# Hybrid trunk kernel: the next norm made in the tail of the stage before, and decay rows of the state-space part brought by transfers

## The chip, the cores and the metric

The kernel runs on one core of a Trainium2 chip. The metric is the device time of one launch, in microseconds. The engines are named as in the profile: PE is TensorE, DVE is VectorE, ACT is ScalarE, POOL is GpSimd and SP issues transfers. P is 128 partitions and T is 512 tokens. Activations lie with the features on partitions, so that one "tile" of the residual is 128 features by 512 tokens, and the model width of 1024 is DK = 8 tiles.

## The reference

Two layers of a trunk on 512 tokens of 1024 features, all in fp32. Layer 0 mixes by a state-space part (SSD, 16 heads) beside windowed attention, layer 1 by an mLSTM. Each mixer is followed by an expert layer (`peer`) and a gated embedding:

```python
for i in range(DEPTH):                       # 2
    h = rmsnorm(x, norm_mix[i])
    x = x + (even_mixer if i % 2 == 0 else mlstm_mixer)(h, ...)
    x = x + peer(rmsnorm(x, norm_ffn[i]), pk_w_q[i], ..., pk_u[i], pk_v[i])
    gate = sigmoid(rmsnorm(x, norm_ple[i]) @ ple_gate[i])
    x = x + gate * (p[i] @ ple_w[i])
return rmsnorm(x, norm_final)
```

A norm is `x * rsqrt(mean(x*x) + eps) * g`. In the SSD part the kernel uses the quadratic form over all 512 tokens: for each head n the weights are `exp(cum[t] - cum[s])` for s <= t, times the product of the state inputs, and `y` is these weights times `x * dt`. `cum` is the running sum of the head's decay, one row of 512 numbers per head.

## The kernel before

**Units.** Every fp32 product is made of three products of halves: a value is split into `hi` (rounded) and `lo` (the rest). One unit is a weight block of 128x1024: SP loads it (`w_raw`), ACT makes `w_hi` (`split_hi`, L157), DVE or POOL makes `w_lo` (L163, L170), and PE multiplies it with the activation's halves in 24 matmuls of 512 columns (`product`, L184). Two split buffers let the halves of the next unit be made while PE works on this one.

**Blocks.** The program is a chain of blocks (`together`), each with a barrier of all engines at its end: the start; EvenFront with EvenSSD; the expert layer of layer 0 (TopK, Decode, Gates, Values, Ple); OddMixer; the expert layer of layer 1, which ends in the final norm. Within a block each engine runs its part of the stages in written order; waits are on counted semaphores.

**Norms.** `Norm` works tile by tile: `act_tile` makes the `hi` of x times the gain (L295) and the square (L300), `dve_tile` the `lo` (L312). The sum of squares over features is a matmul with ones: per tile (`pe_sum`, L324), or POOL adds the tiles (`pool_sums`, L333) and PE does one (`pe_total`, L339). Then `act_root` scales the sum (L305) and takes the square root (L307), and DVE takes the reciprocal (L318). The scale is applied to a unit's result, so that PE's units don't wait for it. TopK, OddMixer and the first block begin with `pe_unit`: unit 0, where each of the 8 tiles waits for its `lo` and is followed by the sum of the tile before. All of this stands at the head of the block, after the barrier.

**EvenSSD.** Sixteen heads are worked in pairs, one pair c per step `it` of a loop from -1 to 8. For each head n of pair it+1: PE spreads row n of `decay_rows` (16x512) over 128 partitions by a matmul with a column of the identity (L808, into PSUM bank n % 2, after the exps of head n-2); DVE takes its minimum with a column (L946, into `q`); ACT makes ten exps of 128x128 with a bias, six from the PSUM row (L867) and four from the minimum (L871), into one of R = 3 buffers `ssd_weights`. PE then transposes x of pair it+1 (L814) for `x_dt` (DVE, L961). For `it` in 0 to 4 and 8 PE does one output unit of the attention part (`UNIT_AT`; ACT and DVE make the halves of the unit after it). DVE multiplies the exps of the pair `it` with the mask product (L955, 128x1280), PE does the pair's product (L827, 2 heads x 4 matmuls), DVE adds and gates it (L971, L973), ACT squares it and makes its hi (L879, L880), and PE adds the square by a matmul with ones (L834). Then come root and reciprocal, and the last eight output units, each followed by DVE's scaling (L990) and addition to the residual (L992).

## Time and profile before

| | us |
|---|---|
| median of 3 runs | 4336.39 (4335.25 to 4337.31) |
| the profiled execution | 4336.64 |
| its span in the trace | 4335.1 |
| PE busy in it | 4245.1 (98%) |
| DVE busy in it | 2735.5 (63%) |
| ACT busy in it | 2065.7 (48%) |
| POOL busy in it | 1270.8 (29%) |
| one `w_hi` on ACT (L157, mean of 694) | 1.059 |
| one `w_lo` on DVE (L163, mean of 585) | 1.230 |

The granted clock of PE over the span is 0.99 of full speed. PE has work almost all the time, so the span is made of PE's matmuls and of the few places in which PE waits or runs at the lower clock. Those places are the SSD loop (about 299 to 411 us) and the heads of the blocks (TopK of layer 0 at 457, OddMixer at 2104, TopK of layer 1 at 2670, the final norm at 4312).

### The profile page before, as it was taken

The page shows a single profiled execution, that of the slowest core. Times are in us where ns is not written, and L with a number is a line of the kernel's source. Part 1 is how long each engine was busy: PE and PEld are TensorE (multiplying, and loading weights), DVE is VectorE, ACT ScalarE, POOL GpSimd, SP SyncE. Part 2 cuts the span into 40 slices and gives each one's busy share as a digit, 9 for nine tenths or more (in the row PEclk, how much of TensorE's full clock was granted, in tenths as well). Part 3 has the DMA queues.
Part 4 walks back from the last instruction along what each step waited for, and adds up shares of the span by engine and source line. Part 5 has one row for each costly group of instructions (what it writes and reads, how often), then busy time and mean ns, then how long its engine had stood idle before and what let it go on. Part 6 is the DMA issues. An engine that isn't in the chain of part 4 may idle for free. (4 is left out here: it accounts for less than half of the span.)

```text
span 4335.1 us, 61169 instructions
## 1 busy us (share of the span) xinstructions
PE 4245.1 (98%) x19253; PEld 3441.9 (79%) x19253; DVE 2735.5 (63%) x5672; ACT 2065.7 (48%) x4035; POOL 1270.8 (29%) x1592
## 2 busy tenths in 40 slices
PE   8999999999999999999899999999999999999998
PEld 6665787888888888888688887888888888888886
DVE  3646799677774444444677774997777744444445
ACT  3744333677773333333455553334778743333334
POOL 0300245777770000001100000446888720000002
PEclk9989999999999999999999999999999999999999
DMA  3111233555557555552222222335555575555532
GB/s 113 59 44 40 97 111 135 206 185 181 202 207 253 195 191 196 186 201 97 71 84 85 87 82 90 112 124 175 204 181 203 184 270 193 195 190 194 193 136 83
DMA packets 180220, 654.06 MB, mean 151 GB/s; under 512 B 17424, under 2 KB 17552, under 8 KB 175200
## 3 DMA queue, kind: packets, MB, share of 16 engines
q1 hardware_dynamic: 102960, 371.41, 25.3%
q0 software_dynamic: 40240, 213.69, 13.9%
q10 hardware_dynamic: 36864, 67.13, 4.1%
q8 instruction: 68, 1.11, 0.1%
q14 instruction: 88, 0.72, 0.1%
HBM read 507.42 MB, written 144.74 MB: 150 GB/s over the span
## 5 line engine op out<-in xcount | busy, mean ns | idle before, releaser
L184 PE MATMUL ps<-h_hi,w_hi 128*128 128x512 f32 x4104 | 1621.1, 395 | 38.2 <-DVE h_lo L312 17.8
L184 PE MATMUL ps<-h_hi,w_lo 128*128 128x512 f32 x4104 | 1601.9, 390 | 0.0
L184 PE MATMUL ps<-h_lo,w_hi 128*128 128x512 f32 x4104 | 1601.6, 390 | 0.0
L163 DVE TENSOR_TENSOR w_lo<-w_raw,w_hi 128x1024 fp32r<-128x1024 f32 x585 | 719.3, 1230 | 1089.9 <-ACT w_hi L157 1085.5
L157 ACT ACTIVATE w_hi<-w_raw 128x1024 fp32r<-128x1024 f32 x694 | 734.8, 1059 | 1029.6 <-PE ps L184 878.2
L184 PEld LDWEIGHTS ps<-h_hi,w_hi 128*128 128x128 f32 x4104 | 771.9, 188 | 213.6 <-issue 40.3
L184 PEld LDWEIGHTS ps<-h_hi,w_lo 128*128 128x128 f32 x4104 | 771.8, 188 | 164.1
L184 PEld LDWEIGHTS ps<-h_lo,w_hi 128*128 128x128 f32 x4104 | 772.3, 188 | 154.9 <-issue 4.3
L1490 POOL TENSOR_SCALAR second_hot<-iota,token_keys 128x128 fp32r<-128x128 f32 x1024 | 723.7, 722 | 0.0
L184 PE MATMUL ps<-y_hi,w_hi 128*128 128x512 f32 x1344 | 534.1, 397 | 12.2 <-DVE y_lo L312 10.3
L1528 ACT ACTIVATE first_scaled<-first_hot,token_keys 128x128 fp32r<-128x128 f32 x1792 | 539.4, 388 | 3.2 <-issue 2.6
L184 PE MATMUL ps<-y_lo,w_hi 128*128 128x512 f32 x1344 | 525.8, 391 | 0.0
L184 PE MATMUL ps<-y_hi,w_lo 128*128 128x512 f32 x1344 | 525.7, 391 | 0.0
L170 POOL TENSOR_TENSOR w_lo<-w_raw,w_hi 128x1024 fp32r<-128x1024 f32 x109 | 279.8, 2567 | 699.2 <-ACT w_hi L157 699.2
L1599 POOL DMA_DIRECT2D gelu_block<-acts x30 | 26.5, 883 | 1188.4 <-DVE y_lo L1626 612.4
L184 PEld LDWEIGHTS ps<-y_hi,w_hi 128*128 128x128 f32 x1344 | 254.2, 189 | 72.5 <-issue 11.4
L1438 DVE TENSOR_REDUCE gate_group<-ps 128x512 f32<-128x1024 f32 x256 | 302.6, 1216 | 6.3 <-PE ps L1509 6.3
L1459 DVE TENSOR_SCALAR first_hot<-iota,token_keys 128x128 f32<-128x128 f32 x1024 | 242.1, 303 | 91.2 <-PE ps L1509 51.7
L184 PEld LDWEIGHTS ps<-y_lo,w_hi 128*128 128x128 f32 x1344 | 254.0, 189 | 56.0 <-issue 4.0
L184 PEld LDWEIGHTS ps<-y_hi,w_lo 128*128 128x128 f32 x1344 | 253.8, 189 | 53.3
L1021 ACT ACTIVATE gelu<-ps 128x512 f32<-128x512 f32 x256 | 151.1, 590 | 281.7 <-PE ps L184 281.3
L1609 ACT ACTIVATE h_hi<-gelu_block 128x512 fp32r<-128x512 f32 x128 | 81.0, 633 | 251.9 <-DVE gelu_block L1621 251.9
(333 smaller groups left out, 3562.6 us busy)
## 6 DMA issues: line engine op xcount, KB each, us to landing
w_raw<-in_u SPq DMA_DIRECT2D x256, 512.0 KB, 3.3
w_raw<-in_v SPq DMA_DIRECT2D x256, 512.0 KB, 3.3
gates<-gate_group POOLq DMA_DIRECT2D x36, 2048.0 KB, 8.3
acts<-gelu ACTq DMA_DIRECT2D x256, 256.0 KB, 2.1
gate_block<-gates POOLq DMA_DIRECT2D x32, 2048.0 KB, 17.8
gelu_block<-acts POOLq DMA_DIRECT2D x30, 2048.0 KB, 11.4
w_raw<-in_od_in SPq DMA_DIRECT2D x65, 512.0 KB, 3.2
w_raw<-in_ev_in SPq DMA_DIRECT2D x33, 512.0 KB, 3.3
```

Source lines behind the costliest of these rows:

```text
L157: self.nc.scalar.activation(self.wh[:, slot % SPL, :], self.raw[:, slot, :], ACT.Copy).then_inc(self.sig("w_hi_ready").sem, 1)
L163: self.nc.vector.tensor_tensor(self.wl[:, slot % SPL, :], self.raw[:, slot, :], self.wh[:, slot % SPL, :].bitcast(F32), ALU.subtract).then ...
L170: self.nc.gpsimd.tensor_tensor(self.wl[:, slot % SPL, :], self.raw[:, slot, :], self.wh[:, slot % SPL, :].bitcast(F32), ALU.subtract).then ...
L184: ins = self.nc.tensor.matmul(out, a[:, s, w], b[:, k, :], start=first and j == 0 and m == 0, stop=last and j == n - 1 and m == 2)
L1021: p.nc.scalar.activation(self.ga[:, s, :], p.ps[:, s, :], ACT.Gelu).then_inc(self.ge.sem, 1)
L1438: v.tensor_reduce(gb[:, half, :, at:at + 4].rearrange("p a t -> p t a"), self.bank(q).rearrange("p t c a -> p t a c"), AX_X, ALU.add).then ...
L1459: ins = v.tensor_scalar(o1[:, t % R1, :], p.iota[:, :], self.key(0, t), None, ALU.is_equal)
L1490: ins = p.nc.gpsimd.tensor_scalar(self.o2[:, t % self.R, :], p.iota[:, :], self.key(1, t), None, ALU.is_equal)
L1528: ins = p.nc.scalar.activation(self.os[:, t % self.R, c, :], self.o1[:, t % self.R1, :], ACT.Copy, scale=self.key(2 + c, t))
L1599: pool.dma_start(at[:, 1 - s, :, :], rows[:, bass.ds(i * B + B, B), :]).then_inc(bl[1 - s].sem, 16)
L1609: self.p.nc.scalar.activation(self.halves[s][0][:, j, :], self.at[:, s, j, :], ACT.Copy).then_inc(self.ah.sem, 1)
```

## The change

**Seams.** The tiles of the next norm are made in the tail of the block before it: as soon as the residual's tile is final, ACT makes its `hi` and square, DVE its `lo`, POOL adds the square to a total, and PE does one matmul with ones at the end of the block. This goes for EvenSSD (norm of expert layer 0), Ple of layer 0 (norm of the mLSTM) and OddMixer (norm of expert layer 1). The next block begins with a plain `product` and `act_root`. Since `hi` and `lo` are written while the block's last units still read the other pair, layer 1 swaps the pairs h and y.

**Root.** `act_root` makes a dummy square root of a column of ones ahead of its wait, in all norms.

**Decay rows.** Only heads 0 and 1 are still spread by PE. POOL writes `decay_rows` to DRAM, and loads each row n >= 2 spread over 128 partitions into a ring of four tiles of `xbc` that are free by then. Rows 2 to 5 are loaded at once, row n >= 6 after the exps of head n-4. DVE's minimum and ACT's six exps read the row from SBUF. The squares of the SSD output are summed on POOL, and PE does one matmul with ones at the end, not eight.

```diff
@@ Norm
     def act_root(self, act):
         a, ps = self.p.nc.scalar, self.p.ps
+        a.activation(self.p.spare[:, :], self.p.ones[:, 0:1], ACT.Sqrt)
         act.wait_ge(self.ss.sem, self.ss.at(DK))
@@ EvenSSD
+    def row(self, n):
+        return self.p.ps[:, n, :] if n < 2 else self.b["xbc"][:, 8 + n % self.RING, CONV - 1:]
@@ EvenSSD.gpsimd
+        pool.wait_ge(self.rc.sem, self.rc.at(1))
+        pool.dma_start(self.held, self.cum[:, :]).then_inc(self.kept.sem, 16)
+        pool.wait_ge(self.kept.sem, self.kept.at(16))
+        def load(n):
+            if n >= 2 + self.RING:
+                pool.wait_ge(self.ex.sem, self.ex.at(n - self.RING + 1))
+            pool.dma_start(self.row(n), self.held[n:n + 1, :].to_broadcast([P, T])
+                           ).then_inc(self.loaded[n % self.RING].sem, 16)
+        pool.wait_ge(self.cb.sem, self.cb.at(2))
+        for n in (2, 3):
+            load(n)
+        for it in range(DK + 1):
+            for n in (2 * it + 4, 2 * it + 5):
+                if n < HEADS:
+                    load(n)
+            c = it - 1
+            if c >= 1:
+                pool.wait_ge(self.sq.sem, self.sq.at(c + 1))
+                if c > 1:
+                    pool.wait_ge(self.sa.sem, self.sa.at(c - 1))
+                g.tensor_tensor(self.total, self.s2[:, 0, :] if c == 1 else self.total,
+                                self.s2[:, c % 2, :], ALU.add).then_inc(self.sa.sem, 1)
+        pool.wait_ge(self.osc.sem, self.osc.at(1))
+        self.after.pool_sums(pool)
@@ EvenSSD.tensor
                 for n in (2 * c, 2 * c + 1):
-                    if n >= 2:
-                        pe.wait_ge(self.ex.sem, self.ex.at(n - 1))
-                    t.matmul(p.ps[:, n % 2, :], p.ident[0:H, n:n + 1].to_broadcast([H, P]), self.cum[:, :],
-                             start=True, stop=True).then_inc(self.sp.sem, 1)
+                    if n < 2:
+                        t.matmul(self.row(n), ...).then_inc(self.sp.sem, 1)
...
-            for c in ((it - 2,) if it < DK else (it - 2, it - 1)):
-                if c >= 0:
-                    pe.wait_ge(self.sq.sem, self.sq.at(c + 1))
-                    t.matmul(p.ps[:, 3, :], p.ones[:, :], self.s2[:, c % 2, :], start=c == 0, stop=c == DK - 1
-                             ).then_inc(self.ss.sem, 1)
+        pe.wait_ge(self.sa.sem, self.sa.at(DK - 1))
+        t.matmul(p.ps[:, 3, :], p.ones[:, :], self.total, start=True, stop=True).then_inc(self.ss.sem, 1)
         pe.wait_ge(self.zl.sem, self.zl.at(DK))
         for k in range(DK, 2 * DK):
             unit(k)
+        self.after.pe_total(pe)
@@ EvenSSD.scalar
-                                         p.ps[:, n % 2, j * P:(j + 1) * P], ACT.Exp,
+                                         self.row(n)[:, j * P:(j + 1) * P], ACT.Exp,
...
+            act.wait_ge(self.osc.sem, self.osc.at(k - DK))
+            self.after.act_tile(act, k - 1 - DK)
@@ EvenSSD.vector
+                        got = self.loaded[n % self.RING]
+                        dve.wait_ge(got.sem, got.at(16 * ((n - 2) // self.RING + 1)))
                         dve.wait_ge(self.ex.sem, self.ex.at(n - 1))
...
+            if i:
+                self.after.dve_tile(dve, i - 1)
             dve.wait_ge(used.sem, u0 + k + 1)
@@ TopK.tensor
-        self.norm.pe_unit(pe, u0, p.ps[:, 4, :])
-        for n in range(1, L):
-            query(u0 + n, (u0 + n) % RAW, 4 + n, (p.yh, p.yl))
+        for n in range(L):
+            query(u0 + n, (u0 + n) % RAW, 4 + n, (self.norm.hi, self.norm.lo))
@@ TopK.scalar
-        for k in range(DK):
-            self.norm.act_tile(act, k)
-            if k == 3:
-                split(1)
+        split(1)
         self.norm.act_root(act)
@@ Ple.scalar
-            if self.final and i:
+            if i:
                 act.wait_ge(self.ad.sem, self.ad.at(i))
                 self.last.act_tile(act, i - 1)
@@ Ple.vector
+            if i >= 2 and not self.final:
+                self.last.dve_tile(dve, i - 2)
@@ OddMixer.tensor
-        self.norm.pe_unit(pe, self.u0, p.ps[:, 7, :])
+        p.product(pe, self.u0, self.u0 % RAW, p.ps[:, 7, :], p.hh, p.hl).then_inc(used.sem, 1)
...
+        self.after.pe_total(pe)
```

On PE, in a step of the SSD loop of the kernel before, between the products of one pair (L827) and the next output unit (L184):

```order
L827 MATMUL ps<-ssd_weights,x_dt 64x512
L827 MATMUL ps<-ssd_weights,x_dt 64x384
L827 MATMUL ps<-ssd_weights,x_dt 64x256
L827 MATMUL ps<-ssd_weights,x_dt 64x128
L808 MATMUL ps<-decay_rows,ident 128x512 x2
L814 MATMUL ps<-ident,xbc 128x128 x4
L184 MATMUL ps<-y_hi,w_hi 128x512
```

The same place of the changed kernel:

```order
L864 MATMUL ps<-ssd_weights,x_dt 64x512
L864 MATMUL ps<-ssd_weights,x_dt 64x384
L864 MATMUL ps<-ssd_weights,x_dt 64x256
L864 MATMUL ps<-ssd_weights,x_dt 64x128
L851 MATMUL ps<-ident,xbc 128x128 x4
L185 MATMUL ps<-y_hi,w_hi 128x512
```

The two spreads (L808) are gone, and with them PE's wait for the exps; nothing else changed places.

On POOL, before, from the SSD part's two small steps to the end of the block (the branches are the barrier):

```order
L756 COPY incl_centred<-incl 128x128 [waits ssd_turned]
L758 TENSOR_TENSOR incl_centred<-incl_centred,ones 64x128 [waits ssd_centred]
L191 UNCONDITIONAL_BRANCH
L207 UNCONDITIONAL_BRANCH [waits barrier_Pool_Activation_PE_DVE_SP_gather]
L1178 UNCONDITIONAL_BRANCH
```

And in the changed kernel, where L772 is the write of the rows to DRAM, L778 are the loads, L793 the adds of the SSD output's squares and L335 those of the next norm:

```order
L770 TENSOR_TENSOR incl_centred<-incl_centred,ones 64x128 [waits ssd_centred]
L772 DMA gates<-decay_rows 16x512 [waits ssd_rows]
L778 DMA xbc<-gates 128x512 [waits ssd_cb,ssd_rows_kept]
L778 DMA xbc<-gates 128x512 x3
L778 DMA xbc<-gates 128x512 [waits ssd_exp] x4
L793 TENSOR_TENSOR q<-squares 128x512 [waits ssd_squares]
L778 DMA xbc<-gates 128x512 [waits ssd_exp] x2
L793 TENSOR_TENSOR q<-q,squares 128x512 [waits ssd_squares_added,ssd_squares]
L778 DMA xbc<-gates 128x512 [waits ssd_exp] x2
```

An idle engine got a queue in which the loads of a pair stand behind the add of an earlier pair's square.

On PE at the seam into TopK of layer 0, before (the branches are the barrier; `pair_sums` holds the squares):

```order
L184 MATMUL ps<-h_hi,w_lo 128x512
L191 UNCONDITIONAL_BRANCH
L197 UNCONDITIONAL_BRANCH
L184 MATMUL ps<-y_hi,w_hi 128x512
L184 MATMUL ps<-y_lo,w_hi 128x512
L184 MATMUL ps<-y_hi,w_lo 128x512
L324 MATMUL ps<-pair_sums,ones 128x512
```

And in the changed kernel:

```order
L185 MATMUL ps<-h_hi,w_lo 128x512
L341 MATMUL ps<-q,ones 128x512
L192 UNCONDITIONAL_BRANCH
L198 UNCONDITIONAL_BRANCH
L185 MATMUL ps<-y_hi,w_hi 128x512
L185 MATMUL ps<-y_lo,w_hi 128x512
L185 MATMUL ps<-y_hi,w_lo 128x512
```

The eight sums of one tile each, which stood between the matmuls of the block's unit 0, became one, ahead of the barrier.

## Rows read from the trace of the kernel before

**Rows 1.** The page's groups: op, shape, count | busy, mean ns | PE's idle time before, releaser.

```profile
L184 PE MATMUL ps<-h_hi,w_hi 128*128 128x512 f32 x4104 | 1621.1, 395 | 38.2 <-DVE h_lo L312 17.8
```

**Rows 2.** Timeline of PE, 311 to 383 us: start, duration, instructions [idle before <-releaser].

```profile
311.11 0.78 PE L184 MATMUL ps<-y_hi,w_hi 128*128 128x512 f32 x1
...
319.19 3.93 PE L827 MATMUL ps<-ssd_weights,x_dt 128*64 128x512 f32 x16
...
365.11 1.98 PE L808 MATMUL ps<-decay_rows,ident 16*128 16x512 f32 x4
367.02 0.66 PE L814 MATMUL ps<-ident,xbc 128*128 128x128 f32 x4
...
382.25 6.71 PE L827 MATMUL ps<-ssd_weights,x_dt 128*64 128x512 f32 x16 [1.69 <-DVE ssd_weights L955]
```

**Rows 3.** PE by windows from one L827 to a next: us, busy (instructions), clock, DMA.

```profile
333.25:347.30 14.05, 13.70 (x49) 0.88 0.12 38
...
360.20:373.08 12.88, 12.88 (x51) 1.00 0.13 41
373.08:382.25 9.17, 7.48 (x28) 0.94 0.00 0
382.25:394.19 11.94, 10.26 (x26) 0.76 0.00 0
394.19:400.75 6.56, 6.56 (x19) 0.74 0.00 0
```

**Rows 4.** Timeline of ACT, exps of head 0, and of DVE, `x_dt` of pair 0.

```profile
302.77 1.66 ACT L867 ACTIVATE ssd_weights<-ps,decay_biases 128x128 f32<-128x128 f32 x6
304.29 1.30 ACT L871 ACTIVATE ssd_weights<-q,decay_biases 128x128 f32<-128x128 f32 x4
```

```profile
303.36 0.75 DVE L961 TENSOR_TENSOR x_dt<-ps,dt_cols 128x256 f32<-128x256 f32 x2 [0.35 <-PE ps L814]
```

**Rows 5.** The tile ssd_weights: ns min/median/max, first and last start.

```profile
L955 DVE TENSOR_TENSOR ssd_weights<-ssd_weights,q x16: 1479/1484/1493, 312.2 to 401.1; 128x1280 f32<-128x1280 f32 x16
```

**Rows 6.** Landing of OddMixer's row loads (tile od_row), and the page's gate_block loads.

```profile
DMA to landing us min/median/max: 3.2/3.3/4.4
```

```profile
gate_block<-gates POOLq DMA_DIRECT2D x32, 2048.0 KB, 17.8
```

**Rows 7.** Timeline at the seam into TopK of layer 0.

```profile
457.52 0.69 DVE L992 TENSOR_TENSOR residual<-ssd_out,residual 128x512 f32<-128x512 f32 x1
...
460.68 0.77 PE L184 MATMUL ps<-y_hi,w_hi 128*128 128x512 f32 x1 [3.92 <-DVE y_lo L312]
...
477.95 0.60 ACT L305 ACTIVATE peer_scores_left<-ps 128x512 f32<-128x512 f32 x1 [2.46 <-PE ps L324]
```

**Rows 8.** Timeline at the seam into OddMixer, then PE's waits of 2126 to 2160.

```profile
2109.27 0.77 PE L184 MATMUL ps<-h_hi,w_hi 128*128 128x512 f32 x1 [5.34 <-DVE h_lo L312]
...
2126.59 0.60 ACT L305 ACTIVATE rstd<-ps 128x512 f32<-128x512 f32 x1 [2.49 <-PE ps L324]
```

```profile
PE ps L184 <- POOL w_lo L170: 3.9, 2, 3.3
```

**Rows 9.** Timeline at the seam into TopK of layer 1.

```profile
2673.31 0.47 PE L184 MATMUL ps<-y_hi,w_hi 128*128 128x512 f32 x1 [3.26 <-DVE y_lo L312]
...
2687.87 0.60 ACT L305 ACTIVATE peer_scores_left<-ps 128x512 f32<-128x512 f32 x1 [2.48 <-PE ps L324]
```

**Rows 10.** Timeline of the final norm.

```profile
4319.00 2.05 PE L339 MATMUL ps<-squares_total,ones 128*128 128x512 f32 x2 [6.19 <-POOL squares_total L333]
...
4321.70 1.28 ACT L307 ACT_TABLE_LOAD   x1
```

**Rows 11.** Lines L1359 (DVE, two SBUF inputs) and L333 (POOL add): ns min/median/max.

```profile
L1359 DVE TENSOR_TENSOR pos_equal<-pos_float,iota x16: 2291/2293/4373, 696.3 to 2965.1; 128x2048 f32<-128x2048 f32 x16
```

```profile
L333 POOL TENSOR_TENSOR squares_total<-squares_total,squares x18: 1260/1852/1857, 2023.5 to 4317.6; 128x512 f32<-128x512 f32 x18
```

More of the change, by code:

```diff
@@ L1038, with __init__ @@
     N = 4 * PEER_HEADS + 4
-    def __init__(self, p, b, rows, wq, us, sub, gain, nxt, ctx):
+    def __init__(self, p, b, rows, wq, us, sub, before, hn, nxt, ctx):
         H = PEER_HEADS
@@ L1708, with __init__ @@
     EMB_AT = 5
-    def __init__(self, p, values, emb, gate, gain, nxt, ctx, final=None):
+    def __init__(self, p, values, emb, gate, gain, pairs, nxt, ctx, final=None, then=None):
         self.p, self.values, self.src, self.gate, self.nxt, self.final = p, values, emb, gate, nxt, final
@@ L1721, in __init__ @@
         self.ld, self.hi, self.lo, self.et, self.sc, self.si, self.mu, self.ad = (Mark(p.sig(n), k) for n, k in counts)
+        if then:
+            self.last = Norm(p, then, pairs[1], 6, scratch=(self.norm.s2, None), total=total)
         if final:
@@ L2131, in scalar @@
         hi(HEADS, 1, DK - 1)
-        for k in range(2, 2 * DK):
-            ahead(k)
+        for k in range(2, 2 * DK + 1):
+            if k < 2 * DK:
+                ahead(k)
+            half, q = OUT_UNITS[k - 1]
+            if half == 1:
+                act.wait_ge(self.added.sem, self.added.at(q + 1))
+                self.after.act_tile(act, q)
     def vector(self, dve):
@@ L2225, in weigh @@
                           ).then_inc(self.vs.sem, 1)
-        for k in range(DK):
-            self.norm.dve_tile(dve, k)
         self.norm.dve_root(dve)
@@ L2317, in ffn_firsts, with ffn @@
     return firsts(d[f"wq{layer}"])
-def ffn(p, layer, nxt, final=None):
+def ffn(p, layer, before, hn, nxt, final=None, then=None):
     d = p.dram
```

119 lines of the change are left out of this document (68 added, 51 removed).

## Prediction, made before the changed kernel ran

> **What bounds the kernel now.** First the table of the profile: PE is busy 98% of the span, so only two kinds of time can go: matmuls that are no longer there or run at a higher clock, and waits of PE. The page's costliest group [rows 1], PE's units, says what the longest wait is for: of its 38.2 us of idle time, 17.8 are spent on `h_lo`, the half that the next norm makes at the head of a block. The change works on three seams, the final norm and the SSD loop, which I read apart.
>
> In the SSD loop the timeline of PE [rows 2] and its windows [rows 3] show the period from one pair's products to the next: 14.05 us for two steps, 12.9 for two, then 9.2, 11.9, 6.6 and 4.7. The first four hold an output unit and PE is busy in 13.7 of 14.05 and in all of 12.9: PE itself is the bound. In the next two PE idles 1.7 us each and runs at a clock of 0.94 and 0.76 of full speed. At the lower of its two levels (1.2 against 2.4 GHz, granted 0.5) the pair's product takes 6.71 us in place of 3.93 [rows 2].
>
> **SSD loop, PE's part.** A spread pair takes 1.91 us warm (365.11 to 367.02 in [rows 2]), the product 3.86 (3.93 less its overlap), the transposes 0.66, and a unit 24 x 0.227 = 5.45, the rest of the 12.88 of a step with spread and square sum [rows 3]: 3.86 + 1.91 + 0.66 + 5.45 = 11.88, and 1.0 for the square's matmul. Without the spreads and the sum, PE's step is 3.86 + 0.66 + 5.45 = 10.0 us.
>
> **SSD loop, the chain behind it.** Three weight buffers mean that a head's exps wait for the product of the head three before. The way round is: half a product 1.95, handoff 0.5, ten exps, the square and hi of ACT (1.3, two operations of 0.6 and 0.7), `w_hi` 1.06, `w_lo` 1.23 (table of the profile) and the multiplication 1.48 [rows 5]. The exps: six of the PSUM row cost 1.52 us from start to start [rows 4], 0.25 each; four from SBUF come to about 1.16, 0.29 each. Six from SBUF cost 6 x 0.04 = 0.24 more, so 2.95 in all. Sum 1.95 + 0.5 + 2.95 + 1.3 + 1.06 + 1.23 + 1.48 = 10.5, of which ACT's hi and DVE's work partly overlap: I take 10.2. PE and chain are level, so the four steps with units become 10.1 each: 53.9 (twice 14.05 and twice 12.9) less 40.4 = 13.5 us gained.
>
> The steps without a unit (three of them, and the last with less): ACT needs 2 x 2.95 + 1.3 = 7.2, and DVE with two multiplications, x_dt and five operations of 128x512 (0.7 each, as in [rows 7]) about the same. I take 7.5, 7.5, 6.0 and 4.0 in place of 9.15, 11.95, 6.55 and 4.7: 7.35. The head of the loop: unit 2 starts at 311.11 behind the spreads of heads 2 and 3 [rows 2]. Afterwards only x_dt of pair 0 holds the transposes of pair 1: it ends at 304.1 [rows 4], they 0.6 later, so that the unit can start at 304.7, 6.4 earlier; 6 of it I count, since the unit is cold and DVE's multiplications stand behind the exps. One sum of squares less at the end: 1.0. Together 6 + 13.5 + 7.35 + 1.0 = 27.9.
>
> **What the loop gives back.** PE will idle 3 of 7.5 us in steps 5 to 7, where it idled 1.7 of 9.2 and 11.9 and the clock had already fallen to 0.74 to 0.94. I expect the lower level from there through the unit behind the loop: product 6.7 + transposes 1.1 = 7.8, slightly above the chain's 7.5, and about 5 us on units 7 and 8. That is 6 us. Second, POOL now adds squares (1.26 to 1.86 us each, median 1.85 [rows 11]), and DVE's minimum reads the row from SBUF. The same rows show a DVE operation with two SBUF inputs at 2.29 us and once 4.37 beside POOL. One such wait a step on part of eight steps: 1.3 us. So the loop gives 27.9 - 7.3 = 20.6; bounds 13 (cold in the steps with units as well) and 27 (no clock loss).
>
> The Trainium skill ("SBUF — State Buffer", section "Who interferes with whom") says that a DVE instruction with two SBUF inputs contends with a GpSimd instruction that reads SBUF, and that the lock is exclusive. The row of 4.37 agrees. By that rule each of 14 minima could wait out a whole POOL add, 14 x 1.2 = 17 us; since only one of 16 instances in the row shows it in full and a POOL add fills 1.3 to 1.9 of 7.5 to 10 us, I keep 1.3.
>
> **The new wait.** DVE now waits for a row's landing, and with it its multiplications, x_dt and gating, then ACT's exps and PE. The loads of OddMixer are of the same shape (one DRAM row over 128 partitions, 256 KB) and land in 3.2 to 4.4 us [rows 6]. A row n is asked for after the exps of head n-4 and used after those of n-2, a pair later: 10 us in the steps with a unit, 7.5 without. POOL's queue puts the add of a square ahead of the loads, so there remain some 7 us: enough, but by 1 to 2 us only for the last pairs. I count nothing, and up to 2 us in the range.
>
> **Seams.** The way over each seam after: last residual tile, ACT hi and square 1.3, POOL add 1.3 to 1.9, ones matmul 1.0 warm or 2.05 cold, barrier 0.6, unit 5.45 warm, 7.5 cold for its first part. Seam 1: today the residual is ready at 457.52 + 0.69 = 458.2 and unit 0 with its sums is over at 477.95 [rows 7]: 19.7 us. After: 1.3 + 1.5 + 2.05 + 0.6 + 7.5 = 13.0 (POOL idle, so that only the last add counts): gain 6.7, taken as 6.5. Seam 2: from the last matmul, 5.34 of wait and 2126.59 - 2109.27 = 17.3 [rows 8], 22.7 us. After, the final norm is the model, which already works in this way: 6.19 of wait and 2.05 for the matmul [rows 10], 0.7 more for hi, 0.6 and 7.5: 17.0, gain 5.7. Here the root is ready some 13 us earlier too, and POOL's `w_lo` no longer holds PE for 3.9 us [rows 8] (this is work behind ACT, whose root and table load come late today); I count 3.3 of it. Seam 2: 9.0. Seam 3: 3.26 + 14.56 = 17.8 today at full clock [rows 9]; after, 0.8 for the eviction + 1.3 + 1.6 + 1.5 + 0.6 + 6.7 (between warm and cold) = 12.5: gain 5.3. The sum of seams is 20.8; bounds 13 (cold throughout, no wait gone) and 25. In the tails the new steps lie beside units of 5.45 us on engines busy about half the time; this cover costs nothing.
>
> **Roots.** The dummy square root moves one table load of 1.28 us [rows 10] off the chain at the end: 1.3. At the start the same load stands ahead of the first root, and PE has no other work queued behind it for long; I count 1.2 there, with 0 as the lower end. In the seams it is hidden. Together 2.5. The Trainium skill ("ScalarE: Activation LUTs", section "What ACT_TABLE_LOAD costs") puts a switch at 2.66 us with its drain; by that the end would gain 2.7. In the trace the square root starts 0.01 us behind the load, so I stay with the row.
>
> **The sum.** 20.6 + 20.8 + 2.5 = 43.9 us. From the profiled execution's 4336.6 that is 4292.7; its median lies 0.25 lower, so 4292.5.
>
> **Rivals.** (A) The clock stays low through most of the SSD loop: with the spreads gone PE no longer fills the steps with units, since the chain (10.2) is longer than its work (10.0), and a unit at 1.2 GHz costs 10.3 in place of 5.45. For it: 0.88 and 0.76 in [rows 3]. Against: 1.00 where PE was busy throughout. Four steps at 12 give 7.5 less: 4300. (B) The seams keep half: PE idles 5 us in one piece and the following unit is cold all along, 10.3 us each, and the waits for `w_lo` stay: 10.5 less, 4303. For it: the cold 2.05 of [rows 10]; against: unit 0 is cold today as well. (C) The chain ACT, DVE, PE doesn't shorten as I sum it, since handoffs or the port hold each step at 12 with the unit and 9 without: 12 less, 4305. (D) Slower: the rows land late. In the six pairs loaded in the loop each microsecond beyond some 7 us of landing costs one per pair. To eat 43.9 us the landing must be 7 + 7.3 = 14.3 us; if it were 17.8 as the gate loads' [rows 6], the loss is 6 x 10.8 = 65 and the time 4358. For it: it is one source row read by 128 partitions, through POOL's queue; against: the same shape lands in 3.3. (E) Next to nothing: what the loop gains is lost to A and C together, what the seams gain to B, leaving under 8 us: 4329 or more.
>
> **Chances.** Forecast 0.54, A 0.16, B 0.12, C 0.11, E 0.04, D 0.03. The range: at best the loop gives 27 and the seams 25 with 2.5 of roots and 2 for what I can't see, 4279; at the other end A with B or C, 4311. That holds over 0.8. A difference of 0.2%, 8.7 us, is about what a measurement of this kernel can tell from none: faster than that 0.93, within it 0.04, slower 0.03.
>
> **What would show it.** In the profile after: no L808-like spreads but two in the loop; the periods between the pairs' products 10 with a unit and 7 to 8 without; the waits for `h_lo` and `y_lo` gone at 2.1 and 2.7 ms, and in their place one wait of about 3 to 6 us for the POOL sum ahead of each block's last matmul; table load ahead of the sum at the end. A DVE minimum that waits for a load, or PE windows with a clock of 0.5 in the steps with units, would prove the forecast wrong towards D or A; a unit 0 of 10 us after a seam towards B; exps or minima stretched beside POOL towards C.

## The result, and the profile after

The changed kernel takes 4291.94 us (median of 4 runs, 4291.61 to 4292.42) where the kernel before takes 4336.01 (4335.25 to 4337.31): a ratio of 0.9899, 95% interval 0.9884 to 0.9914, or 44.1 us less. The forecast was 4292.5 with a range of 4279 to 4311. The total was hit within 0.6 us, which is luck: the terms behind it were off by up to 2.6 us each, with both signs, and this cancelled. One more run of the changed kernel gave 4293.71 (see the clock in the first stage), so that even its own times differ by more than 0.6.

The waits of PE over the whole span, after (us in total, times, longest), with [rows 1], [rows 7] and [rows 8] to compare:

```profile
PE ps L341 <- POOL squares_total L335: 17.6, 2, 11.4
PE ps L864 <- DVE ssd_weights L996: 11.0, 7, 4.4
PE ps L185 <- DVE h_lo L314: 10.5, 2, 10.0
PE ps L185 <- POOL w_lo L171: 8.4, 9, 2.1
...
PE ps L341 <- POOL q L335: 4.3, 1, 4.3
...
PE ps L341 <- POOL od_kT L335: 3.5, 1, 3.5
```

The waits for `h_lo` and `y_lo` at the seams are gone; the 10.5 us that remain are at the program's start. In their place stand waits for POOL's sum, one at each seam (4.3, 11.4, 3.5) and 6.2 at the end. In the SSD loop PE waits 11.0 us for the multiplied exps, not 3.4 as before.

PE's products of one pair in the SSD loop, after, which answer to [rows 2]:

```profile
312.54 3.90 PE L864 MATMUL ps<-ssd_weights,x_dt 128*64 128x512 f32 x16 [0.27 <-DVE ssd_weights L996]
...
343.16 3.90 PE L864 MATMUL ps<-ssd_weights,x_dt 128*64 128x512 f32 x16 [0.40 <-DVE ssd_weights L996]
...
353.52 3.90 PE L864 MATMUL ps<-ssd_weights,x_dt 128*64 128x512 f32 x16 [0.39 <-DVE ssd_weights L996]
...
362.41 5.57 PE L864 MATMUL ps<-ssd_weights,x_dt 128*64 128x512 f32 x16 [4.40 <-DVE ssd_weights L996]
...
372.98 7.97 PE L864 MATMUL ps<-ssd_weights,x_dt 128*64 128x512 f32 x24 [4.42 <-DVE ssd_weights L996]
...
390.29 1.12 PE L869 MATMUL ps<-q,ones 128*128 128x512 f32 x2 [0.53 <-POOL q L793]
```

The steps with a unit take 10.4 us (the first 9.87) where they took 12.9 to 14.05, and PE's waits of 0.4 us in them say that the chain, not PE, is now the bound by that little. Part of this gain is the clock's: the two steps of 14.05 ran at 0.88 of full speed [rows 3], and all four run at full speed now. The steps without a unit take 8.89 and 10.57 us, and PE waits 4.4 us in each.

PE by windows, after (window, us, busy and instructions, granted clock, DMA), answering to [rows 3]:

```profile
353.52:362.41 8.89, 4.49 (x21) 1.00 0.32 92
362.41:372.98 10.57, 6.15 (x21) 0.84 0.21 45
372.98:384.09 11.11, 10.28 (x33) 0.85 0.00 0
```

The seams, after: PE's sum ahead of the barrier, and the first matmul behind it, at the three places of [rows 7 to 9], and the end ([rows 10]):

```profile
439.31 2.04 PE L341 MATMUL ps<-q,ones 128*128 128x512 f32 x2 [4.33 <-POOL q L335]
...
441.69 0.77 PE L185 MATMUL ps<-y_hi,w_hi 128*128 128x512 f32 x1 [0.33 <-PEq L192]
```

```profile
2087.27 2.04 PE L341 MATMUL ps<-squares_total,ones 128*128 128x512 f32 x2 [11.39 <-POOL squares_total L335]
...
2089.64 0.76 PE L185 MATMUL ps<-h_hi,w_hi 128*128 128x512 f32 x1 [0.33 <-PEq L192]
```

```profile
2637.26 2.05 PE L341 MATMUL ps<-od_kT,ones 128*128 128x512 f32 x2 [3.54 <-POOL od_kT L335]
```

```profile
4274.08 1.28 ACT L305 ACT_TABLE_LOAD   x1
4275.37 0.20 ACT L305 ACTIVATE spare<-ones 128x1 f32<-128x1 f32 x1
...
4278.15 0.60 ACT L307 ACTIVATE gate_block<-ps 128x512 f32<-128x512 f32 x1 [2.58 <-PE ps L341]
4278.78 0.63 ACT L309 ACTIVATE gate_block<-gate_block 128x512 f32<-128x512 f32 x1
```

At the end the table load now lies in ACT's wait, and the square root starts 0.03 us behind the scaling.

**Where the time went.** ACT makes the `w_hi` of the same unit in both kernels, 694 of them, so that their start times compare place by place (negative: the changed kernel is ahead):

| place | before, us | after, us | ahead by | gained since | forecast |
|---|---|---|---|---|---|
| start, unit 4 | 40.2 | 38.1 | -2.1 | 2.1 | 1.2 |
| SSD loop's first exps, unit 35 | 308.1 | 308.6 | +0.5 | -2.6 | 0 |
| behind the loop, unit 41 | 411.6 | 389.9 | -21.7 | 22.2 | 20.6 |
| seam 1, unit 51 | 485.8 | 456.3 | -29.6 | 7.8 | 6.5 |
| end of TopK, unit 90 | 717.1 | 688.6 | -28.6 | -1.0 | 0 |
| tail of the embedding stage, unit 327 | 2082.3 | 2054.3 | -28.0 | -0.6 | 0 |
| the same, unit 330 | 2098.6 | 2073.3 | -25.3 | -2.7 | 0 |
| seam 2, unit 337 | 2176.6 | 2141.6 | -35.0 | 9.7 | 9.0 with the row above |
| end of OddMixer's units, unit 409 | 2653.6 | 2617.5 | -36.1 | 1.1 | 0 |
| seam 3, unit 414 | 2695.7 | 2654.3 | -41.4 | 5.3 | 5.3 |
| last expert rows, unit 685 | 4266.2 | 4223.2 | -43.0 | 1.6 | 0 |
| end of the span | 4335.1 | 4290.9 | -44.2 | 1.2 | 1.3 |

The 1.0 us lost in TopK is a fall of the clock for 3.4 us at 663 us (0.57 over 663 to 667), which the kernel before doesn't have. From unit 51 to unit 90 it takes 231.3 us and the changed kernel 232.3. In the traces of all runs below, the stretch takes 232.3 where the clock falls in it, and 231.3 to 231.5 where it doesn't (the SSD loop alone, the last square by PE, both edits).

### The profile page after: what moved, and what is told of

Read it like the earlier page. It is cut to its first block and busy times, and to the rows that moved or that the text cites. A ratio compares the mean times of both kernels' runs of the same rounds, so it can differ in the third digit from the quotient of the medians.

```text
span 4290.9 us, 61077 instructions
## 1 busy us (share of the span) xinstructions
PE 4199.3 (98%) x19169; PEld 3427.7 (80%) x19169; DVE 2744.5 (64%) x5672; ACT 2068.8 (48%) x4042; POOL 1312.7 (31%) x1635
## 5 line engine op out<-in xcount | busy, mean ns | idle before, releaser
L185 PE MATMUL ps<-h_hi,w_hi 128*128 128x512 f32 x3080 | 1216.3, 395 | 22.4 <-DVE h_lo L314 10.5
L185 PE MATMUL ps<-h_hi,w_lo 128*128 128x512 f32 x3080 | 1203.1, 391 | 0.0
L185 PE MATMUL ps<-h_lo,w_hi 128*128 128x512 f32 x3080 | 1202.4, 390 | 0.0
L185 PE MATMUL ps<-y_hi,w_hi 128*128 128x512 f32 x2368 | 928.9, 392 | 7.3 <-POOL w_lo L171 4.1
L185 PE MATMUL ps<-y_hi,w_lo 128*128 128x512 f32 x2368 | 924.9, 391 | 0.0
L185 PE MATMUL ps<-y_lo,w_hi 128*128 128x512 f32 x2368 | 924.5, 390 | 0.0
L185 PEld LDWEIGHTS ps<-h_hi,w_lo 128*128 128x128 f32 x3080 | 579.9, 188 | 123.4
L185 PEld LDWEIGHTS ps<-y_hi,w_hi 128*128 128x128 f32 x2368 | 446.8, 189 | 103.1 <-issue 7.6
L185 PEld LDWEIGHTS ps<-y_hi,w_lo 128*128 128x128 f32 x2368 | 446.0, 188 | 94.7
L185 PEld LDWEIGHTS ps<-y_lo,w_hi 128*128 128x128 f32 x2368 | 446.4, 189 | 89.7
## 6 DMA issues: line engine op xcount, KB each, us to landing
gelu_block<-acts POOLq DMA_DIRECT2D x30, 2048.0 KB, 11.6
```

Source lines behind the costliest of these rows:

```text
L185: ins = self.nc.tensor.matmul(out, a[:, s, w], b[:, k, :], start=first and j == 0 and m == 0, stop=last and j == n - 1 and m == 2)
```

## The experiments

All runs are compared with runs of the kernel before on the same chip, whose medians were 4335.9 to 4336.6. Intervals of the ratios are about 0.0017 to either side, 7 us; for smaller differences I go by the medians of 4 runs, which lie within 1 to 3 us, and by the traces. The runs were taken on three chips, so that a difference of 2 us between two edits isn't told by medians alone.

### The three parts apart

**The SSD loop alone.** The kernel before with the SSD hunks of the diff (rows by transfers, squares summed by POOL), and none of the rest.

> The kernel before with the decay rows by transfers and the squares of the SSD output summed by POOL, and nothing else of the change: the seams and the roots are as before. Theory (the sum of the prediction, corrected by the trace after): from the first spread to output unit 8 the changed kernel takes 91.5 us in place of 113.8, so this part alone gives 22 us: 4314. Rival: the loop profits from the seams' edits to the squares' buffer or the halves, or its gain is eaten behind it (unit 8 to the seam): 10 to 15 us, 4321 to 4326.

4314.14 us (4313.65 to 4316.15), ratio 0.9950 (0.9934 to 0.9967): 22 us, as the theory had it. The periods of the loop are those of the changed kernel with a unit (10.36) and in step 5 (8.89), but steps 6 and 7 take 11.03 and 6.09 us, against 10.57 and 5.64 (PE by windows, steps 5 and 6):

```profile
351.91:360.80 8.89, 4.49 (x21) 0.95 0.32 91
360.80:371.83 11.03, 7.40 (x20) 0.65 0.18 42
```

The clock falls earlier here (0.95 over step 5, where the changed kernel has 1.00, and 0.65 over step 6, against 0.84), and the product between the two steps takes 6.81 us in place of 5.57. This is the first sign that PE's clock bears on step 6, and it takes away the ground of the rival stated below for the idle time filled, that both kernels had equal periods. What is gained in the loop is kept: it is 22.4 us ahead behind the loop and 22.9 at the end.

**The seams alone.** The changed kernel with the SSD part as before and without the early root.

> The kernel before with the three seams made ahead and nothing else: spreads by PE, no square root ahead of its sum. Theory: 8 us at the first seam, 7 at the second, 5 at the third: 20 us, 4316. Without the early root each seam's reciprocal comes 1.3 us later, which PE does not see. Rival: the seams need the early root, since the first evictions of the next block wait for the reciprocal: 3 us less in all, 4319.

4316.76 us (4314.12 to 4317.33), ratio 0.9953 (0.9936 to 0.9969): 19.6 us.

**The early root alone.** The kernel before with

```diff
+        a.activation(self.p.spare[:, :], self.p.ones[:, 0:1], ACT.Sqrt)
         act.wait_ge(self.ss.sem, self.ss.at(DK))
```

> The kernel before with the square root of a column of ones ahead of each norm's wait and nothing else. Prediction's step: 1.3 us at the end and 1.2 at the start, 4333.5. Rival, from the trace after: in the changed kernel PE is 2.1 us ahead at 263 us and 1.1 us behind at the first spread, since the granted clock fell to half at 271 to 274 us, where it stayed full before. If this fall comes with the shift of 2 us itself, the start's gain turns into a loss of 1 us and the whole gives 0 to 1 us: 4335 to 4336. If the fall has another cause, 4333.

4327.05 us (10 runs, 4325.79 to 4329.69), ratio 0.9980 (0.9971 to 0.9990): both expectations missed, the gain is 9 us. The ten runs lie in two groups (4325.8 to 4326.1 and 4328.0 to 4329.7), and the profiled one is in the upper, so that its trace has to account for 7.4 us. By the same comparison of `w_hi` it is 1.9 us ahead at 40 us, 0.7 behind at 308, 2.2 ahead behind the loop, 3.3 ahead at the head of OddMixer and 4.6 behind its root, 5.9 at 3320 and 7.4 at the end. So in the kernel before the roots of seam 2 and of the end stood on the path by their full 1.3 us. Of the 2.9 us gained in the SSD loop 1.6 lie in one step, that of the second pair, where the clock stayed at full and had not before [rows 3]:

```profile
332.97:345.42 12.45, 12.10 (x49) 1.00 0.13 43
```

The rest lies in steps of under 1.3 us that I can't assign.

**The changed kernel without the early root.** The one line taken out.

> The changed kernel without the square root of a column of ones ahead of each norm's wait. Loop alone gave 22 us, seams alone 20, roots alone 9, together 51, but the changed kernel gains 44. Theory: with the sum made ahead the root at a seam is early enough in any case, so that the roots give only 1.3 us at the end and 1 to 2 at the start: 2.5 us slower than the changed kernel, 4294.5. Rival: the roots give the same 7 to 9 us here, and it is the seams and the loop that overlap: 4299 to 4301.

4295.52 us (4295.13 to 4296.05), 3.6 more than the changed kernel's median, and 1.8 more than its single run on the same chip (4293.71). So behind a sum made ahead the root is worth 2 to 4 us, not 9. The theory's number holds, but only half of its places: by `w_hi` the early root's 1.7 us at the start have shrunk to 0.3 behind the SSD loop; it is 1.5 us ahead at unit 337, 0.8 at seam 3, 2.1 at the last unit, and the end gives the 1.3.

The parts alone give 22.2 + 19.6 + 9.3 = 51 us, together 44. By `w_hi` the sum of the three parts is more than the changed kernel's gain by 3.1 us up to the end of the SSD loop (22.4 + 0.2 + 2.2 against 21.7), by 1.9 at seam 1 and by 2.9 at seam 2, and less by 1.0 in TopK and by 2.6 at seam 3. The first is not the roots at the seams. Both the early root alone and the seams alone have the second pair's step at 12.45 us in place of 14.05, and the SSD loop of the changed kernel takes the same time away. The others I can place only roughly: a sum made ahead hides the root's 1.3 us at seam 2, and the clock falls at different times in each kernel.

### What holds the loop now

**Rows that land later.** In the changed kernel each row is loaded, awaited and loaded again:

```diff
-            pool.dma_start(self.row(n), ...).then_inc(self.loaded[n % self.RING].sem, 16)
+            for again in range(2):
+                pool.dma_start(self.row(n), ...).then_inc(got.sem, 16)
+                if not again:
+                    pool.wait_ge(got.sem, got.at(32 * ((n - 2) // self.RING) + 16))
```

> The changed kernel, but each decay row is loaded, waited for on POOL and loaded again before DVE may read it: a row lands some 4 to 5 us later (two transfers of 3.3 to 6.5 us in place of one), and POOL's queue holds the next load for that time. Theory of the prediction: rows have a lead of about 7 us over 3.3 to 4.4 of landing, 10 us between the pairs in the steps with a unit. So two landings in a row (9 to 10 us, and 18 to 20 for a pair, since POOL waits in between) must show: the period of the steps goes from 10.4 to the 18 to 20 us that POOL needs for two rows, six pairs, 45 to 60 us slower: 4340 to 4350, above the kernel before. Rival: the lead is longer than thought, DVE's minimum waits little, and the time is within 15 us of 4292.

4303.90 us (4301.98 to 4305.05): 12 us more, where my theory said 48 to 58. The rival within 15 us holds. The timeline of DVE in this kernel shows the new wait:

```profile
310.69 0.69 DVE L991 TENSOR_TENSOR q<-xbc,decay_cols 128x512 f32<-128x512 f32 x1 [4.40 <-DMA xbc<-gates]
...
322.95 0.69 DVE L991 TENSOR_TENSOR q<-xbc,decay_cols 128x512 f32<-128x512 f32 x1 [5.77 <-DMA xbc<-gates]
```

POOL's next load follows the landing at once, so a row takes 6 us here and a pair 12, not 18 to 20: the first load of a row is issued together with the second of the row before (two issues in 1.06 us). A pair every 12 us against the chain's 10.4 costs 2 a step. In the changed kernel itself rows land in 3.3 to 6.5 us (median 4.4), longer than the 3.2 to 4.4 of [rows 6], and no minimum waits for one: the trace's list of DVE's idle time ahead of the minima names the exps (11.6 us) and the spreads of the first two heads (1.1), no transfer. The lead is enough: in the trace of the changed kernel rows lie ready 1.7 to 12 us before their minimum starts, and from row 10 on, where POOL's add stands ahead of the loads, 1.7 to 3.5 us. In this run the rate of POOL's queue holds the loop, not one row's way, so it doesn't measure the lead by itself; it does show that a row that is there some 9 us after its first issue leaves the kernel faster than before.

**The squares on PE again.** The eight matmuls with ones back in the loop, no POOL adds in it:

> The changed kernel with the SSD output's squares summed by PE again (eight matmuls with ones, one a step), no POOL adds in the loop. In the trace after, the multiplications at 359.70 and 370.27 take 3.96 us for two where the others take 2.88, and POOL adds a square at that very time. Theory (port): without the adds these are 2.9 again, the two steps without a unit become 1.1 us shorter each, but PE does 8 matmuls of 1.05 us more, which count in the four steps with units only as far as PE is the bound (10.0 against a chain of 10.36: 0.3 to 0.7 each) and at the end (1 us): 0 to 2 us slower in all, 4292 to 4294. Rival (the sum on PE costs its full 8 us, since PE bounds the loop): 4297 or more. Other rival: the POOL adds hold the row loads behind them, and without them the loop is 4 us or more faster: 4288.

4291.83 us (4290.65 to 4292.59): unchanged, and the two effects that should cancel are both there. DVE's multiplications, in the changed kernel (steps 4 and 5) and in this one (step 5):

```profile
351.89 2.88 DVE L996 TENSOR_TENSOR ssd_weights<-ssd_weights,q 128x1280 f32<-128x1280 f32 x2
...
359.70 3.96 DVE L996 TENSOR_TENSOR ssd_weights<-ssd_weights,q 128x1280 f32<-128x1280 f32 x2
```

```profile
360.08 2.89 DVE L992 TENSOR_TENSOR ssd_weights<-ssd_weights,q 128x1280 f32<-128x1280 f32 x2
```

And POOL in the changed kernel:

```profile
359.59 1.31 POOL L793 TENSOR_TENSOR q<-q,squares 128x512 f32<-128x512 f32 x1 [7.97 <-ACT squares L914]
...
380.74 2.05 POOL L793 TENSOR_TENSOR q<-q,squares 128x512 f32<-128x512 f32 x1 [9.26 <-ACT squares L914]
```

A multiplication with two SBUF inputs that is issued while POOL adds waits for nearly the whole rest of the add: the pair takes 3.96 us in place of 2.88, 1.1 us more, with 1.2 us of the add left. So it is in steps 5 and 6 of every kernel here that has the adds there, except the one with rows loaded twice, where the two don't meet. The steps of 8.89 and 10.57 become 7.83 and 9.51. Against that, the steps with a unit become 10.8 at two places, where PE's matmul with ones makes PE the bound again, and step 7 takes 6.55 us in place of 5.64. It is the rule of the Trainium skill ("SBUF — State Buffer", "Who interferes with whom") at work, and it works both ways: the add at 359.59 was not stretched, since it had come first, while the one at 380.74, issued 0.57 us after a multiplication of 1.49 us (L996 at 380.17), took 2.05.

**PE's idle time filled.** Useless matmuls ahead of the pair's products in steps 5, 6 and 7:

```diff
+            if it in (5, 6, 7):
+                for k in range(16 if it < 7 else 4):
+                    t.matmul(p.ps[:, 0, :], p.yh[:, k % DK, 0:P], p.yh[:, k % DK, :], start=k == 0, stop=k == 15,
+                             skip_group_check=True)
```

> The changed kernel with matmuls without use (16, 16 and 4 of 512 columns, of y's hi with itself, into a free bank) ahead of the pair's products in the steps 5, 6 and 7 of the SSD loop, where PE waits 4.4, 4.4 and 0.8 us. They fill 3.6 us of each wait. Theory of the prediction's clock term: with PE busy the granted clock stays at full, the products take 3.9 us in place of 5.6 to 7, the exps behind their first half start 1.5 to 2 us earlier, and the steps 6 and 7 shorten by about 2 us each: 4 us gained, 4288. Rival: the chain of ACT and DVE sets these steps whatever PE's clock, as the equal periods of 8.89 and 10.57 us in two kernels with clocks of 1.00 and 0.84 against 0.86 and 0.66 suggest: 4292, unchanged.

4288.63 us (4287.37 to 4290.44): 3.3 us less, as the clock term had it. PE's products in this kernel:

```profile
362.29 3.90 PE L868 MATMUL ps<-ssd_weights,x_dt 128*64 128x512 f32 x16 [0.79 <-DVE ssd_weights L1000]
371.20 3.90 PE L868 MATMUL ps<-ssd_weights,x_dt 128*64 128x512 f32 x16 [0.78 <-DVE ssd_weights L1000]
376.84 3.90 PE L868 MATMUL ps<-ssd_weights,x_dt 128*64 128x512 f32 x16 [0.61 <-DVE ssd_weights L1000]
```

Step 5 is as long as in the changed kernel (8.92), step 6 takes 8.91 in place of 10.57, and step 7 5.64 as before; from the start of the last pair's product to the first matmul behind it there are 3.83 us in place of 5.40. These two make the 3.3 us. A product that runs at 1.2 GHz for part or all of its time (5.57 to 6.81 us in these traces) stands in the chain, because the next exps wait for its first half; at 2.4 GHz it takes 3.90.

### What holds the seams now

**The order in the embedding stage's tail.**

```diff
@@ Ple.scalar, after the sigmoid of tile i
-            if i:
-                act.wait_ge(self.ad.sem, self.ad.at(i))
-                self.last.act_tile(act, i - 1)
+            if i >= 2:
+                act.wait_ge(self.ad.sem, self.ad.at(i - 1))
+                self.last.act_tile(act, i - 2)
@@ Ple.vector, after the scaling of tile i
-            if i >= 2 and not self.final:
-                self.last.dve_tile(dve, i - 2)
             if i:
                 add(i - 1)
+            if i >= 3 and not self.final:
+                self.last.dve_tile(dve, i - 3)
```

The tiles that are left follow behind the loop in the same order.

> The changed kernel with one order changed in the embedding stage ahead of the second seam and of the end: ACT makes the next norm's tile i-2, not i-1, after the sigmoid of tile i, and DVE makes its lo of tile i-3 after the addition, not that of i-2 ahead of it. Theory: in the changed kernel ACT and DVE go round in 6.32 us (w_lo 1.47, scale, lo, product, addition, then ACT's hi, square and w_hi), PE's units in 5.45, so that DVE is 5 us behind at the end and PE waits 11.4 us for the sum at this seam. With the order changed the round is open, and the wait falls to 6 to 7 us: 5 us gained, 4287. At the end of the program nothing to 1 us changes. Rival: the round is held by POOL's adds beside DVE (w_lo at 1.47 in place of 1.23) or by the number of operations, and the order changes nothing: 4292.

4290.31 us (4288.51 to 4291.35): 1.6 us less by the medians, too little to tell apart by them alone. The trace tells: the wait of PE for the sum fell from 11.39 to 7.93 us, and ACT's and DVE's round from 6.32 to 5.44. In the changed kernel (timeline, one round):

```profile
2053.14 0.72 ACT L296 ACTIVATE h_hi<-residual,params 128x512 fp32r<-128x512 f32 x1 [1.35 <-DVE residual L1880]
2053.77 0.62 ACT L301 ACTIVATE squares<-residual 128x512 f32<-128x512 f32 x1
2054.29 1.04 ACT L158 ACTIVATE w_hi<-w_raw 128x1024 fp32r<-128x1024 f32 x1
...
2055.37 1.47 DVE L164 TENSOR_TENSOR w_lo<-w_raw,w_hi 128x1024 fp32r<-128x1024 f32 x1 [2.26 <-ACT w_hi L158]
2056.76 0.68 DVE L1891 TENSOR_TENSOR gelu_block<-ps,rstd 128x512 f32<-128x512 f32 x1
2057.36 0.74 DVE L314 SCALAR_TENSOR_TENSOR h_lo<-residual,params,h_hi 128x512 fp32r<-128x512 f32 x1
```

Each operation waits for the one above it: `w_hi` stands behind the norm's hi and square of the tile before, these wait for DVE's addition, and that stands behind `w_lo`. PE, two units ahead, doesn't wait meanwhile, so the list of its waits shows the whole lag only at the block's end. Of the 5 us the mended order gave 3.5 at the seam; three lo's of DVE were left for the end, where they run beside POOL's adds (4.08 us for three in place of 2.2). By `w_hi` it gains 9.9 us from unit 327 to unit 337 where the changed kernel gains 7.0. Two things work against it in the whole: the steps 6 and 7 of the SSD loop took 11.04 and 6.09 us in this trace (10.57 and 5.64), where the edit changes nothing, and at the end of the program PE waited 7.00 us for the sum in place of 6.18.

**The last square by PE.**

```diff
@@ Norm.pool_sums
-        for k in range(1, DK):
+        for k in range(1, DK - 1):
@@ Norm.pe_total
-        pe.wait_ge(self.sa.sem, self.sa.at(DK - 1))
-        p.nc.tensor.matmul(..., p.ones[:, :], self.total, start=True, stop=True).then_inc(self.ss.sem, DK)
+        pe.wait_ge(self.sa.sem, self.sa.at(DK - 2))
+        p.nc.tensor.matmul(..., p.ones[:, :], self.total, start=True, stop=False)
+        pe.wait_ge(self.sq.sem, self.sq.at(DK))
+        p.nc.tensor.matmul(..., p.ones[:, :], self.s2[:, (DK - 1) % 2, :], start=False, stop=True
+                           ).then_inc(self.ss.sem, DK)
```

> The changed kernel where POOL adds only seven squares of a norm, and PE takes the eighth by a matmul with ones of its own, into the same sum: in the three seams, the embedding stages and the final norm. It tests what the last POOL add (1.3 to 1.9 us, at the final norm two in a row in 3.1) costs on the path. Theory: at each seam and at the end the sum is ready 1.3 to 1.9 us earlier, and of PE's two matmuls one lies in the wait: 4 x 1.5 = 6 us gained, 4286. Rival: PE's second matmul at half clock (2.05 us for one sum in the trace after) eats it, since both matmuls then stand behind the wait: 0 to 1 us, 4291.

4286.32 us (4285.59 to 4288.05): 5.6 us less, the theory's number, but not its four times 1.5 us. PE's sums at seams 3 and 2 in this kernel:

```profile
2630.91 1.02 PE L341 MATMUL ps<-od_kT,ones 128*128 128x512 f32 x2
2633.22 1.10 PE L343 MATMUL ps<-od_tmp,ones 128*128 128x512 f32 x2 [1.29 <-ACT od_tmp L301]
```

```profile
2083.43 2.08 PE L341 MATMUL ps<-squares_total,ones 128*128 128x512 f32 x2 [9.62 <-POOL squares_total L335]
2085.30 1.66 PE L343 MATMUL ps<-squares,ones 128*128 128x512 f32 x2
```

At seams 1 and 3 the first matmul finds its sum ready and cuts PE's wait in two (4.33 us to 2.02, 3.54 to 1.29). At seam 3 the clock then doesn't fall (1.00 over 2626 to 2640 us, where the changed kernel has 0.76 over 2629 to 2643). At these two seams the edit gives 2.4 and 3.9 us by `w_hi`. At seam 2 and at the end POOL is still behind, both matmuls stand behind the wait, as the rival had it, and the edit gives 0.9 us and nothing. In TopK the clock doesn't fall, which gives 0.8. In the two embedding stages, whose own sums aren't waited for, the added matmul costs 0.9 us each. So the last square pays as a matmul where the sum of the others is ready before PE runs out of work, and part of what it pays there is the clock.

**Both, and all four edits.**

> The changed kernel with the order of the embedding stage's tail changed (as in tail_mended) and the last square of each norm taken by PE (as in last_square_on_pe). If the two are of different places, their gains add: 1.6 + 5.6 = 7.2 us, 4284.7. If both take away the same wait, that of PE for POOL's sum at the second seam, where tail_mended left three lo's of DVE beside the last POOL adds, the gain is more than the sum, since the last add there (1.4 us) no longer runs beside them: 4283. If the tail's gain was chance: 4286.3.

4284.82 us (4284.30 to 4285.84), 7.1 us less than the changed kernel: the gains of 1.6 and 5.6 add. At seam 2 the wait is 6.17 us.

> The changed kernel with all four edits: both of both_mended, the SSD squares summed by PE, and eight matmuls without use ahead of the pair's products in each of steps 5 and 6 of the SSD loop. Theory: POOL's adds lengthened two multiplications in steps 5 and 6 by 1.1 us each, and the lower clock lengthened the products behind the waits; with both gone the steps 5 and 6 take about 7.8 us each in place of 8.9 and 10.6, as the prediction's 7.5 had it, and the loop gains 3.5 to 4.5 us less 2 us for the sum's matmuls: with 7.2 of the other edits 4281 to 4283. Rival: port and clock are the same gain taken twice: 4284.

4279.12 us (4278.73 to 4281.62), ratio to the kernel before 0.9870 (0.9854 to 0.9887): the best of both kernels and all edits, 12.8 us under the changed kernel, somewhat more than expected. Of the 5.7 us that it is under the kernel with both edits, the two traces show 4.2, all in the SSD loop; the rest is within what the medians tell. PE's products of a pair, from that which ends step 4 to that which ends step 7:

```profile
355.07 3.93 PE L863 MATMUL ps<-ssd_weights,x_dt 128*64 128x512 f32 x16
...
362.92 3.90 PE L863 MATMUL ps<-ssd_weights,x_dt 128*64 128x512 f32 x16 [0.58 <-DVE ssd_weights L998]
...
370.73 3.90 PE L863 MATMUL ps<-ssd_weights,x_dt 128*64 128x512 f32 x16 [0.59 <-DVE ssd_weights L998]
...
376.37 3.90 PE L863 MATMUL ps<-ssd_weights,x_dt 128*64 128x512 f32 x16 [0.69 <-DVE ssd_weights L998]
```

The steps 5 and 6 take 7.85 and 7.81 us, step 7 5.64: the 7.5, 7.5 and 6.0 of the prediction, which were right for a loop without the port and without the low clock.

### The clock in the first stage

> The changed kernel once more, for the granted clock. In its trace the clock is at half at 271 to 274 us, where the kernel before has it at full, though PE's instructions up to there are the same; the rows of the kernel with the SSD part alone have it at full, those with the seams alone at half. Theory: where the clock falls is fixed by the program and its timing, and the second execution shows the fall at the same place, with PE some 1 us behind the kernel before at the first spread. Rival: it is chance from one execution to the next, and the fall is elsewhere or absent.

4293.71 us (one run). The fall is there again, at nearly the same place (0.66 of full speed over 271 to 274 us, where the first trace has 0.50 and the kernel before 1.00), and PE reaches the first spread at 299.0, 0.2 us behind the kernel before. So it repeats. It appears in the traces of the changed kernel, of all its edits that keep the early root, of the roots alone and of the seams alone (0.74 over 274 to 278 us), and not in those of the kernel before, of the SSD part alone and of the changed kernel without the early root. With the early root PE comes 0.8 to 2.6 us earlier to the same instructions (by `w_hi` at 40 us). But seams alone comes no earlier, and shows it too. What decides it I leave open. What it costs can be read: by `w_hi` the kernels that show it lose 1.0 to 2.6 us against the kernel before between 40 and 308 us, the other two at most 0.1. The second execution differs elsewhere too: step 6 of the SSD loop took 11.04 us in it, and 10.57 in the first.

## Why the prediction was right, point by point

The total was right because misses of both signs cancelled. The mechanisms were those forecast in the steps with a unit and at seams 1 and 3. At seam 2, in the clock's part of the loop and in the count behind the port's term a step of the working was wrong.

- **Steps with a unit**: right. 10.36 us against 10.1, and chain and PE level as stated: 0.4 us of wait, and 10.8 as soon as PE has a matmul more.
- **Steps without a unit**: the times of 7.5 were right for the chain, but not for this kernel. The steps took 8.89 and 10.57. The port was sized at 1.3 us in all and cost 2.1, in just the two steps where the chain is bare; the clock, sized at 6 us, cost 3.3. The two corrections together were 7.3 us in the sum and 5.4 in the runs. The head of the loop gave 7.1 against 6, the steps with a unit 12.9 against 13.5, and the last steps 0.8 less than summed apart from the corrections: 22.2 against 20.6.
- **The clock's term** was too large and lay in the wrong place. The sum put about 5 of its 6 us on units 7 and 8 behind the loop and next to nothing on the products. In the trace unit 7 runs at full speed (0.39 us a matmul), and what the clock cost lies in step 6 and in the last pair's product.
- **The port's term**: the row of 4.37 us was read correctly as a block of the whole POOL operation, but a maximum was taken for a count. The sum says that only one of 16 instances shows it in full. The trace of the kernel before has two in full (4.36 and 4.37) and five more at 3.14 to 3.50 us, seven in all, each issued while POOL made a `w_lo`:

```profile
718.25 2.39 POOL L170 TENSOR_TENSOR w_lo<-w_raw,w_hi 128x1024 fp32r<-128x1024 f32 x1 [3.45 <-ACT w_hi L157]
719.31 3.49 DVE L1359 TENSOR_TENSOR pos_equal<-pos_float,iota 128x2048 f32<-128x2048 f32 x1
```

- The choice of operation was wrong too: I looked at the 14 minima, which met no add, while the 16 multiplications, which the change doesn't touch, have two SBUF inputs too and met two.
- **The new wait for rows** cost nothing, as said. Rival D's working was tried as well: a row awaited twice is there after some 9 us, which by it costs 6 x 2 = 12 us, and 12 were measured. This agrees by luck, since what held the loop there was POOL's queue, at 12 us for a pair. My own expectation of that run, 48 to 58, had put the issues one behind another, where POOL overlaps them.
- **Seam 1** 7.8 against 6.5 and **seam 3** 5.3 against 5.3: right. Both sums took 2.04 us, at the lower clock. The barrier, put at 0.6 us without a row of its own, took 0.33. At seam 3 the clock fell, which it had not in the kernel before; I had taken a value between both.
- **Seam 2** 9.7 less the 2.7 lost ahead of it, 7.0 against 9.0. (The 2.7 is a lag of ACT; PE's last matmul ahead of the seam ends 28.1 us ahead of that of the kernel before, and its units earlier in the stage start 28.6 ahead.) The step that failed is the sentence that the new steps in the tails lie beside units on engines busy half the time, and that this cover costs nothing. It looked at busy shares, not at the order: in the embedding stage they closed a round of 6.32 us, against PE's 5.45, and PE waited 11.39 us for the sum where the working had 6.19. The wait for POOL's `w_lo` fell from 3.9 to 0.3 us, as counted, and of the 2.8 us for `od_gate_rows` 1.6 went as well, which wasn't counted; the wait for `qk_rows` grew from 0.3 to 2.0.
- **The roots**: 1.8 to 3.6 us by the runs without them, against 2.5. The start gave 2.1, not 1.2, and lost more than that to the clock by 308 us, so that hardly anything of the start's term was left.
- **Rivals.** A held in small: low clock in two steps, none in those with units. B held at seam 2, through the round and not the clock. C held in two of eight steps. D's transfer is hidden with room. A and C took 5.4 us of the 7.3 that the sum had set aside for them; B took 2.0, and the clock in the first stage 2.6, for which the sum had nothing. The loop's head and the gains at start and seam 1 made this up.

## What to carry to other kernels

When steps are put "beside" other work, write down the round that they close with what is already there (who waits for whom, in each engine's order) and add it up; a busy share of one half says nothing about it, and the lag shows only at the next barrier. Moving an add to an idle GpSimd was paid for here by VectorE operations with two SBUF inputs that started while it ran, which the change doesn't touch: look for all of them in the stretch, and count instances in the trace, since a maximum doesn't say how often. If a sum must close a stage, the engine that ends it can take the last term itself; this paid where it also broke up that engine's wait, and hardly where the other terms came late.

## What was not expected of the hardware

- Transfers of one row over 128 partitions landed in 3.3 to 6.5 us (median 4.4), beside 3.2 to 4.4 for the same shape in another stage. The longest, 6.1 and 6.5, are the last two of four issued within 2.2 us.
- The early root alone is worth 9 us in the kernel before, by medians. Its trace accounts for 7.4, of which 2.6 are the roots of seam 2 and the end and 1.6 a step of the SSD loop in which the clock no longer fell.
- With one matmul ahead of PE's wait at seam 3, which left 1.3 us of 3.5, the clock did not fall there (1.00 over 14 us, against 0.76 with the whole wait).
- The granted clock fell for 3 us in the first stage in some kernels and not in others with the same instructions on PE up to that point, and it did so again in a second execution.
